# When five small loads are issued, and what a change of TensorE's row mode costs in the planner: a hybrid attention and Fourier layer on eight cores

## The reference

```python
sh_m, sc_m, gt_m, sh_f, sc_f, gt_f = split(silu(c) @ w_ada + b_ada, 6)
h_x = rms_norm(x, g_norm_mix) * (1 + sc_m) + sh_m      # the same for ctx, with c_ctx
q, k, v, f, gates = split(h_x @ w_in)                  # ctx: only k and v
q, k = rope(rms_norm(q, g_q)), rope(rms_norm(k, g_k))  # 16 query heads, 4 key heads, head width 64
attn = softmax(q @ k_all.T / 8) @ v_all                # 2304 keys: latent and context
mix = (sig(g1) * (attn @ w_attn_proj) + sig(g2) * (real(fft2(f)) @ w_fourier_proj)) @ w_o
x = x + gt_m * mix
x = x + gt_f * swiglu(rms_norm(x, g_norm_ffn) * (1 + sc_f) + sh_f)
out = rms_norm(x, g_final)
```

## Time and profile before

| | |
|---|---|
| median of 3 runs | 1551.85 us (1551.61 to 1554.48) |
| the profiled execution | 1549.88 us |
| its span, slowest core (core 0) | 1548.3 us |
| spans of the 8 cores | 1540.3 to 1548.3 us |
| PE busy | 1379.2 us, 89% |
| DVE busy | 889.8 us, 57% |
| ACT busy | 837.5 us, 54% |
| HBM traffic | 126.70 MB read, 16.78 MB written |

### The profile page before, as it was taken

The page is one execution under the profiler, slowest core; times in us unless marked ns, Lnnn a source line. Parts: engine busy times, 40 slices in busy tenths (PEclk is TensorE's granted clock), DMA queues, the critical chain, the costliest instruction groups (busy, mean ns, idle before and its releaser), DMA issues.

```text
span 1548.3 us, 30697 instructions; the slowest of 8 cores (1540.3 to 1548.3 us)
## 1 busy us (share of the span) xinstructions
PE 1379.2 (89%) x9744; PEld 571.2 (37%) x9744; DVE 889.8 (57%) x1409; ACT 837.5 (54%) x1135; POOL 33.1 (2%) x73
## 2 busy tenths in 40 slices
PE   1267887999888988898999999997999999999997
PEld 1155222322223222322223444443444444444443
DVE  2147898898978798878877333376211122123433
ACT  4185988989788888888994222266311111111111
POOL 0000000000000000000000000000000000000000
PEclk9978999999989999999999999999999999999999
DMA  9840000010111212302022043068145233112231
GB/s 219 230 90 1 8 1 2 8 29 2 28 29 31 53 28 56 76 1 49 2 50 49 15 89 102 1 167 275 36 82 102 41 64 55 28 55 82 109 117 74
DMA packets 20464, 98.26 MB, mean 63 GB/s; under 512 B 3153, under 2 KB 3282, under 8 KB 15442
## 3 DMA queue, kind: packets, MB, share of 16 engines
q0 software_dynamic: 5328, 47.19, 16.7%
q1 hardware_dynamic: 14978, 49.11, 9.2%
HBM read 126.70 MB, written 16.78 MB: 93 GB/s over the span
## 4 chain that ended last, share of the span: by engine, by line
PE 67%; ACT 11%; DVE 8%; issue 8%; SPq 4%; DMA 2%; ACTq 0%; DVEq 0%; POOLq 0%; POOL 0%
PE PS L395 51%; PE PS L401 15%; ACT SB L450 10%; DVE SB L454 5%; SPq L294 4%; DMA SB<-x 2%; ACT SB L484 1%; DVE SB L491 1%; PE PS L429 1%; DVE SB L485 1%; DVE SB L470 1%; DVE SB L494 0%; ACTq L286 0%; DVEq L286 0%; DVE SB L468 0%
## 5 line engine op out<-in xcount | busy, mean ns | idle before, releaser
L395 PE MATMUL PS<-SB 128*128 128x512 bf16 x4072 | 975.7, 382 | 12.7 <-DVE SB L454 10.6
L450 ACT ACTIVATE SB<-PS 128x1024 bf16<-128x1024 f32 (+1 forms) x705 | 620.3, 964 | 304.3 <-PE PS L395 252.2
L395 PEld LDWEIGHTS PS<-SB 128*128 128x128 bf16 x4072 | 385.4, 98 | 600.4 <-issue 205.2
L454 DVE TENSOR_TENSOR SB<-SB 128x1024 bf16<-128x1024 bf16 (+5 forms) x659 | 434.0, 685 | 94.1 <-ACT SB L450 63.0
L401 PE MATMUL PS<-SB 64*64 64x512 bf16 (+4 forms) x5236 | 424.1, 373 | 70.5 <-ACT SB L450 40.3
L454 DVE TENSOR_TENSOR SB<-PS,SB 128x512 f32<-128x512 f32 (+3 forms) x262 | 172.7, 674 | 382.1 <-PE PS L395 338.7
L401 PEld LDWEIGHTS PS<-SB 64*64 64x64 bf16 (+1 forms) x5236 | 154.9, 105 | 271.9 <-issue 251.9
L450 ACT ACTIVATE SB<-SB 128x8 f32<-128x8 f32 (+4 forms) x201 | 106.5, 538 | 234.4 <-DVE SB L454 161.7
L450 ACT ACTIVATE SB<-PS,SB 128x512 f32<-128x512 f32 x64 | 44.0, 689 | 137.2 <-PE PS L395 126.6
L491 DVE RECIPROCAL SB<-SB 128x128 f32<-128x128 f32 x128 | 111.0, 915 | 0.6
L429 PE MATMUL PS<-SB 128*128 128x128 bf16 x436 | 41.7, 247 | 76.8 <-DVE SB L454 35.8
(11 more groups left out here) (19 smaller groups left out, 59.1 us busy)
## 6 DMA issues: line engine op xcount, KB each, us to landing
SB<-x SPq DMA_DIRECT2D x32, 512.0 KB, 11.4
SB<-w_ada POOLq DMA_DIRECT2D x12, 1024.0 KB, 8.5
SB<-w_gu POOLq DMA_DIRECT2D x11, 1024.0 KB, 8.3
SB<-w_mix POOLq DMA_DIRECT2D x6, 1792.0 KB, 12.9
x_scratch<-SB SPq DMA_DIRECT2D x16, 512.0 KB, 4.7
SB<-x_scratch SPq DMA_DIRECT2D x16, 512.0 KB, 3.3
out<-SB SPq DMA_DIRECT2D x16, 512.0 KB, 2.6
SB<-w_dn POOLq DMA_DIRECT2D x2, 2048.0 KB, 14.8
```

What stands on the lines that cost most here:

```text
L395: return K.op("pe", lambda h: h.matmul(out.ap, lhsT=lhsT.ap, rhs=rhs.ap, start=start, stop=stop), reads=[lhsT, rhs], writes=[out], cost=ma ...
L450: return K.op("act", lambda h: h.activation(out=out.ap, in_=in_.ap, func=func, **kw), reads=reads, writes=writes, cost=ecost("act", in_), ...
L454: return K.op(eng, lambda h: h.tensor_tensor(out=out.ap, in0=a.ap, in1=b.ap, op=op), reads=[a, b], writes=[out], cost=(1600.0 if op == ALU ...
```

## The change

Two tables and four bias rows get a dependence, and one constant of the planner is larger. `load_tabq(0)` and `load_tabq(1)` wait for the last instruction of `MOD(4)`. The four bias loads of `ada_late_rows` wait for the exponential that last wrote the buffer `PTs[0]`. `SWITCH_NS` goes from 105 to 134. No operation is added or removed. The denominators' products with ones are not touched by the diff.

```diff
-    SWITCH_NS = 105.0
+    SWITCH_NS = 134.0
...
     def load_tabq(qb):
         tq = tabqs[qb % 2]
-        load(tq, ropeq_d[qb].rearrange("p (a b c) -> p a b c", a=4, b=2))
+        load(tq, ropeq_d[qb].rearrange("p (a b c) -> p a b c", a=4, b=2), after=[hchunk(1, 7)] if qb < 2 else [])
...
     def ada_late_rows(gt, v, hf):
         g_half = rng(gt, gt.ap[:, hf * 512:(hf + 1) * 512], hf * 512, hf * 512 + 512, 4)
-        load(g_half, bada_d[v * 1024 + hf * 512:v * 1024 + hf * 512 + 512].partition_broadcast(128))
+        load(g_half, bada_d[v * 1024 + hf * 512:v * 1024 + hf * 512 + 512].partition_broadcast(128), after=[PTs[0]])
```

## The result

The changed kernel takes 1562.23 us (median of 5), against 1551.61 us for the kernel before: ratio 1.0059, interval 1.0034 to 1.0084. It is slower, where 1544.3 us and faster were forecast, and it lies outside the range of 1532 to 1555.5.

What follows compares the result with a forecast made beforehand. PE bounds the whole, but DMA loads through SyncE's queue bound the start, and PE isn't the attention's limit. Loads -6.0, tables +0.5, bias rows 0, order -2 make -7.5: 1551.85 to 1544.3 us; range 1532 to 1555.5.

Steps and rivals of the forecast that it cites:

- What bounds the kernel: Whole kernel: PE 89% busy, but not the limit in the first two slices (DMA engines full) or the attention.
- The moved loads: First stage: 1.57 MB removed ahead of x tile 10 lets it land earlier, -6.0 us, passed on whole.
- the bound by landings: First stage: g_q lands at 63.3 us, the last b_ada at 70.3; all between leaves, 7.0 us.
- The first rival: First stage: keys' Square planned before some late tiles' Squares, gaining up to 12.9 us; total about -14, 1537.5; chance 0.17.
- The tables: After MOD(4): two query tables load beside w_f's packets and DVE may wait; bounds 0 to 4 us, taken +0.5.
- The bias rows: Attention: four bias loads hidden under eight products, cost 0; 3 us kept for the range.
- The order in the attention: Attention: the larger constant places fillers' evictions later in ACT's and DVE's order; bounds -10 to +12 us, taken -2.
- The third rival: Attention: new order puts fillers' evictions ahead of ready exponentials, 2.0 us each; seven more give +8, 1559; chance 0.17.
- the row of 28 waits and 55.3 us: Attention: ACT's waits for a filler's product, 2.0 us each; a quarter shrinking would bring back 3.2 us.

## Why the prediction was wrong

**What bounds the kernel** was right: the start by SyncE's queue, the attention by no engine alone, and the part behind it unchanged (719.6 and 717.4 us on the slowest cores, more than the 1 us allowed, but within the scatter of the cores).

**The moved loads**, -6.0 us, had the right mechanism and were a little too small. Tile 10's Square moved by 10.7 us on the slowest cores compared, the first keys' Square by 9.0, but the slowest core before was a laggard at 84.53. In the median of the eight cores tile 10 lands at 62.1 us in place of 69.4, 7.3 us earlier, just over the bound by landings (7.0), and the first keys' Square is at 73.8 in place of 79.6, 5.8 us earlier. That one pair of traces has its own scatter: the median is 79.6 to 81.8 us in the seven traces with the loads as before, and 72.7 to 74.0 in the six with both groups moved, about 7 us. I had read one core. A range over the eight would have told me that the maximum could move by more. The view of all cores would have shown it.

**The first rival**, the keys' Square moved by up to 12.9 us, didn't come: ACT's order has the late tiles first, as was said against it.

**The tables**, +0.5 us with 4 as the upper end, was mis-sized. DVE waited 2.8 us at least and 11.9 us on the slowest core. I had written that both tables would take up to 9 us under w_f, and then took off DVE's idle 5.49 us, which was the time before the keys' products were ready; it had moved away with them. The rule of the Trainium skill ("DMA: Bandwidth & Descriptors", "Queues, rings and completion order": the engines take turns between queues packet by packet) agrees with the traces: 75 and 74 packets in 4 us on core 2. What I had left out is when the turns begin: not at w_f's issue but with its first packet, 1.2 to 3.8 us later, and by then most packets of a table issued ahead of it have moved.

**The bias rows**, 0 with 3 kept for the range, were right.

**The order in the attention**, "Bounds -10 to +12; I take -2", is the step that failed: it is +15.6 on the slowest core, 16.0 as the constant alone, outside the bounds. The third rival had the side and the kind of the mechanism, ACT's strict order, and 0.17 of the chance; its time of 1559 came from seven more waits of 2.0 us for fillers' products, which didn't come. Three things were wrong in the reasoning. First, the row of 28 waits and 55.3 us reaches to 900 us, past the attention's end at 829; in the stretch to 840 us it is 10 waits and 13.1 us, so the waits I meant to shrink were mostly not there. Second, the term stood on this one kind of wait. It shrank, by 1.9 us, about as forecast; ACT's waits of all kinds in the attention are 90.9 us at 134 where they were 74.0, for DVE's sums and for scores above all, and they had no term. Third, and decisive, I sized the effect from the cost of a mode change (0.11 us against 105 or 134 ns, which I read rightly) as if a small error gave a small effect. 1 ns at one place gives 11.7 us.

One sum was off without consequence: the first rival with the order's whole gain is 1551.85 - 12.9 + 0.5 - 10 = 1529.5 us, not 1532.

## What to carry to other kernels

A constant in a planner that fixes an order by comparing times isn't a quantity with a slope but a new draw: look at the planned length of the stage, measure several neighbours, and keep the order itself once one is good. When a load is moved out of a crowded place, ask what else will be asked for at its new time, on which core, and which of the two comes first: here a few tenths of a us decided 6 to 9 us of landing, and differently on cores that run the same program. A change in two halves that go opposite ways should be taken apart before it is judged; here the loads were worth -0.64% (interval -0.98 to -0.30), the bias rows alone as much (-0.66%), and the constant cost 1.04% (0.34 to 1.75).

## What the runs showed of the hardware

In the run with the tables behind tile 15, cores 2 and 3 of the profiled execution show a granted clock of 0.81 from about 108 to 266 us, but for short pieces at 0.5, neither 1.2 nor 2.4 GHz; core 3, from 180 to 210 us (the clock is the third number from the end):

```profile
180.00:210.00 30.00, 27.82 (x256) 7.80 (x244) 24.47 (x38) 26.80 (x35) 0.00 (x0) 0.81 0.00 1
```

They have 680.9 and 681.7 us of attention at mean clocks of 0.960 and 0.958 over the span. The other six don't show the stretch and have 671.1 to 674.8 us; cores 0 and 1 are at mean clocks of 0.976 and 0.978. With the bias rows alone cores 0 to 3 all have it, from about 110 to 269 us, with a mean clock of 0.960 to 0.962 and 681.4 to 681.9 us, against 669.3 to 675.6 on cores 4 to 7. So such a stretch goes with 6 to 13 us more in a stage of 670, as much as the effects under study, and it falls on some cores alone. What sets it off stays open.
